# Attention heads: three value pairs in one burst, pair sums in the second head's burst, reciprocal in two halves

## The reference

```python
s = jnp.einsum('bqhd,bkhd->bhqk', q, k, preferred_element_type=jnp.float32) * (QK_DIM ** -0.5)
pr = jax.nn.softmax(s, axis=-1).astype(v.dtype)
return jnp.einsum('bhqk,bkhd->bqhd', pr, v)
```

## Time and profile before

| | |
|---|---|
| median of 3 runs | 1334.23 us (1332.66 to 1334.96) |
| profiled execution, its time | 1332.62 us |
| its span, first to last instruction | 1330.8 us |
| busy in the span | PE 1312.5 us, DVE 683.3, ACT 467.9, POOL 433.5 |
| chain that ended last | PE 94%, DVE 3%, DMA 1%, ACT 1% |
| mean granted TensorE clock | 0.993 of full |
| attention heads, first score tile to projection | 278.93 to 368.28 us |

### The profile page before, as it was taken

How to read it: one execution, slowest core, us unless ns; L and a number is a source line. 1 busy time by engine, 2 the same in 40 slices (tenths; PEclk the granted TensorE clock), 3 DMA queues, 4 the chain that set the end, 5 groups by cost and what they waited for, 6 DMA issues and landing times.

```text
span 1330.8 us, 15819 instructions
## 1 busy us (share of the span) xinstructions
PE 1312.5 (99%) x6356; PEld 966.1 (73%) x6356; DVE 683.3 (51%) x1253; ACT 467.9 (35%) x629; POOL 433.5 (33%) x136
## 2 busy tenths in 40 slices
PE   8999999999999999999999999999999999999998
PEld 5789888865578844444447788888888888888887
DVE  2465987767783633333347756712461451551553
ACT  4335222346631221112135671433242341431443
POOL 3143334247712000000015334444245345344340
PEclk9999999999999799999999999999999999999999
DMA  9521199301024799999993113222132222223201
GB/s 374 219 96 64 47 357 328 122 1 64 32 96 190 273 366 420 421 420 421 421 400 127 64 64 127 96 96 95 64 127 95 96 95 95 95 95 103 87 1 64
DMA packets 33924, 226.69 MB, mean 170 GB/s; under 512 B 4000, under 2 KB 4640, under 8 KB 7872
## 3 DMA queue, kind: packets, MB, share of 16 engines
q1 hardware_dynamic: 32416, 218.93, 42.9%
q0 software_dynamic: 1152, 4.19, 0.9%
q10 hardware_dynamic: 288, 2.62, 0.5%
HBM read 221.53 MB, written 4.19 MB: 170 GB/s over the span
## 4 chain that ended last, share of the span: by engine, by line
PE 94%; DVE 3%; DMA 1%; ACT 1%; issue 0%; POOL 0%; SPq 0%; DVEq 0%; ACTq 0%
PE psum L964 24%; PE psum L966 23%; PE psum L965 23%; PE psum L1468 13%; PE psum L1276 1%; PE psum L1242 1%; PE psum L1453 1%; PE psum L1456 1%; DMA raw<-in_stream 1%; PE psum L1540 1%; PE psum L1428 1%; PE psum L1011 1%; DVE rs L2447 1%; PE psum L1016 0%; DVE work L2578 0%
## 5 line engine op out<-in xcount | busy, mean ns | idle before, releaser
L898 POOL TENSOR_TENSOR w_lo<-raw,w_hi 128x2048 fp32r<-128x2048 f32 x79 | 365.2, 4624 | 589.6 <-ACT w_hi L1741 589.6
L964 PE MATMUL psum<-b_hi,w_hi 128*128 128x512 f32 x608 | 238.1, 392 | 0.1
L966 PE MATMUL psum<-b_hi,w_lo 128*128 128x512 f32 x608 | 236.7, 389 | 0.0
L965 PE MATMUL psum<-b_lo,w_hi 128*128 128x512 f32 x608 | 236.6, 389 | 0.0
L1741 ACT ACTIVATE w_hi<-raw 128x2048 fp32r<-128x2048 f32 x80 | 152.6, 1908 | 147.8 <-PE psum L966 101.8
L964 PEld LDWEIGHTS psum<-b_hi,w_hi 128*128 128x128 f32 x608 | 114.1, 188 | 30.7 <-issue 5.7
L966 PEld LDWEIGHTS psum<-b_hi,w_lo 128*128 128x128 f32 x608 | 114.1, 188 | 23.9
L965 PEld LDWEIGHTS psum<-b_lo,w_hi 128*128 128x128 f32 x608 | 114.1, 188 | 23.3
L1468 PE MATMUL psum<-ex_ring,xe 128*64 128x512 f32 x488 | 108.8, 595 | 0.9 <-ACT xe L1966 0.9
L2495 DVE TENSOR_TENSOR x<-psum,x 128x512 f32<-128x512 f32 x39 | 26.9, 692 | 127.9 <-PE psum L966 127.9
L964 PE MATMUL psum<-h_hi,w_hi 128*128 128x512 f32 (+1 forms) x208 | 84.4, 406 | 1.3 <-POOL w_lo L881 1.3
(11 more groups left out here) (432 smaller groups left out, 2294.3 us busy)
## 6 DMA issues: line engine op xcount, KB each, us to landing
raw<-in_stream SPq DMA_DIRECT2D x97, 1024.0 KB, 4.9
ex_ring<-in_stream SPq DMA_DIRECT2D x89, 1024.0 KB, 17.7
mod_in<-in_stream SPq DMA_DIRECT2D x8, 1024.0 KB, 20.7
ex_last<-in_stream SPq DMA_DIRECT2D x7, 1024.0 KB, 17.3
x<-in_x SPq DMA_DIRECT2D x4, 512.0 KB, 7.1
x<-in_x ACTq DMA_DIRECT2D x1, 2048.0 KB, 7.6
xt<-h2t SPq DMA_DIRECT2D x8, 256.0 KB, 10.5
out<-y_out SPq DMA_DIRECT2D x4, 512.0 KB, 3.0
```

The costliest lines, as they stand in the source:

```text
L898: nc.gpsimd.tensor_tensor(w_lo[:, slot, :], raw[:, raw_slot, :], w_hi[:, slot, :].bitcast(F32), ALU.subtract).then_inc(w_lo_done, 1)
L964: mm(o, w[0], x[0], start=start, stop=False)
L965: mm(o, w[0], x[1], start=False, stop=False)
L966: return mm(o, w[1], x[0], start=False, stop=stop)
```

## The change

On TensorE the last value pair of a head moves into the burst behind its own score tiles, which then has three pairs. The sums of a pair of heads follow that burst at the end of heads 1, 3, 5 and 7, in bank 1. On ACT the copy of the sums becomes two copies of 256 columns, behind the row of maxima of heads 1, 3 and 5, ahead of the next head's high parts; the copy of the values' result comes after the second exponential. On VectorE a pair's reciprocal and multiply are made in two halves of 256 tokens, the first at the end of heads 2, 4, 6, the second at the end of heads 3, 5, 7, and both for the last pair after head 7. GpSimd's code is unchanged.

```diff
@@ make_plan
             p.add("sT", h, k, by="act", bank=k % 3)
-            if k == 2 and h >= 2 and h % 2 == 0:
-                p.add("sums", h // 2 - 1, by="act", bank=5)
             if k >= 2 and h + 1 < H:
                 max_pair(h + 1, k - 2)
+        if h % 2 == 1:
+            p.add("sums", h // 2, by="act", bank=1)
         if h + 1 < H:
             p.add("mx_row", h + 1, by="act", bank=0)
@@ tensor
-                    if k == 2 and h >= 1:
-                        pv_pair(h - 1, KT - 2)
-                        if h % 2 == 0:
-                            prob_sums(h // 2 - 1)
                     if k >= 2 and h + 1 < H:
                         max_pair(h + 1, k - 2)
-                pv_pair(h, 0)
-                pv_pair(h, 2)
+                for k in range(0, KT, 2):
+                    pv_pair(h, k)
+                if h % 2 == 1:
+                    prob_sums(h // 2)
                 if h + 1 < H:
                     max_row(h + 1)
...
-            pv_pair(H - 1, KT - 2)
-            prob_sums(H // 2 - 1)
@@ scalar
                 if j >= 1:
-                    act.wait_ge(att_done, j)
-                A(rs[:], o, ACT.Copy).then_inc(freed_act, 1)
+                    act.wait_ge(att_half, j)
+                A(rs_first[:], o[:, 0:FH], ACT.Copy)
+                if j >= 2:
+                    act.wait_ge(att_done, j - 1)
+                A(rs_second[j % 2][:], o[:, FH:T], ACT.Copy).then_inc(freed_act, 1)
...
-                    if k == 2 and h >= 1:
+                    if k == 1 and h >= 1:
                         output(h - 1)
-                        if h % 2 == 0:
-                            output_sums(h // 2 - 1)
...
                 if h + 1 < H:
                     max_row(h + 1)
+                    if h % 2 == 1:
+                        output_sums(h // 2)
@@ vector
+            def pair_output(j, s):
+
+                if s == 0:
+                    dve.wait_ge(freed_act, PLAN.freed_count(TILE["sums", j]))
+                    dve.wait_ge(o_sum, 2 * j + 2)
+                r, tok = (rs_first, rs_second[j % 2])[s], slice(s * FH, s * FH + FH)
+                link(V.reciprocal(r[:], r[:]))
+                V.tensor_tensor(att[:, j, tok], att[:, j, tok], r[:], ALU.mult).then_inc((att_half, att_done)[s], 1)
...
-                if h >= 2 and h % 2 == 0:
-                    pair_output(h // 2 - 1)
+                if h >= 2:
+                    pair_output(h // 2 - 1, h % 2)
...
-            pair_output(H // 2 - 1)
+            for s in range(2):
+                pair_output(H // 2 - 1, s)
```

More of the change, by code:

```diff
@@ L375, in make_plan @@
             head_t(h + 2)
-    p.add("sums", H // 2 - 1, by="act", bank=5)
     p.phase(6)
@@ L591, in build @@
         att = at("att", R + 34, [P, 4, T])
-        rs = at("rs", R + 98, [P, T])
+        rs_first = at("rs_first", R + 98, [P, FH])
+        rs_second = [at("rs_second0", R + 99, [P, FH]), at("rs_second1", R + 31, [P, FH])]
         att_hi = at("att_hi", R + 80, [P, 4, T], F32R)
@@ L731, in build @@
         psum_done = sem("psum_done")
+        att_half = sem("att_half")
         att_done = sem("att_done")
```

## The result

The changed kernel takes 1336.48 us in the median of its 20 runs against 1332.1 us; the ratio is 1.0027 (95% interval 1.0019 to 1.0034), 3.6 us slower. One run took 4632.58 us for a reason that nothing here shows, and is not in the ratio. The profiled execution has a span of 1332.9 us against 1330.8. Spans of one kernel spread by some us. The two traces differ in the granted clock of the routing stage after attention (0.85 from 425 to 444 us in the trace of before, 1.00 in that of after over the same work), and what follows attention took 1.3 us less in that of after. It was 278.93 to 368.28 = 89.35 us and is 279.26 to 371.69 = 92.43 us: +3.08.

A forecast was written before the change was run, and what follows sets the result against it. The prediction took TensorE, busy for 99% of the span, as the bound. Its terms came to +1.14 us, plus 2.06 for held multiplies, so +3.2 on 1334.2 gave 1337.4 us, range 1333.5 to 1340.5.

The forecast's parts named there:

- The lone pair goes: Heads 1, 3, 5, before the burst: without the single value pair TensorE waits for VectorE's low parts; saves 4.76 us.
- Copies ahead of the high parts: Start of heads 2, 4, 6 on ACT: two half copies add 0.72 us; head still saves 1.27 each, 3.81 us.
- t0: Clock of a head: the start of its row of maxima on TensorE (L1255).
- B: Clock of a head: the start of its burst of value products on TensorE (L1276).
- K: End of VectorE's low parts of k in a head; forecast t0+3.90 in odd heads, t0+4.62 in even before meetings.
- Third pair: Bursts of heads 0 to 6: the third value pair adds 0.86 us each, 6.02 us.
- Sums at the end of heads 1, 3, 5: Behind these bursts: sums add 2.58 us, and waiting for GpSimd's fifth addition adds 0.37 three times, 1.11 us.
- rival A: Heads 3 and 5: second-half multiply gets ahead of GpSimd's weight chunk or isn't held; +1.1, 1335.4 us; chance 0.22.
- Where the second halves land: Multiplies of heads 3 and 5 held by GpSimd's weight chunk, delaying heads 4 and 6 by 1.03 us each, +2.06.
- rival B: Not slower: ACT copies and GpSimd's fifth addition hidden, no multiply held; -2.1, 1332.1 us; chance 0.10.
- Head 7, "nothing gained": Last head: the lone pair goes, but the sums wait for GpSimd's additions, so nothing is gained.
- Rival C: More meetings: head 7's half reciprocal and multiply, and later low parts of attention, delay sums; +4.6, 1338.8 us; chance 0.18.

The follow-up runs named there:

- burst_halves_wait: Changed kernel with sums and copies put back, GpSimd waiting for the second half's multiply before weight chunks after heads 3 and 5: 1330.46 us, ratio 0.9983.
- burst_only: Kernel before with only the value pairs' part, three pairs in one burst, sums and whole reciprocal as before: ratio 1.0002.
- after_dve_copies: Changed kernel with GpSimd waiting for the second half's multiply, and the first three pairs' sums copied by VectorE instead of ACT: ratio 1.0007.
- after_pe_fifth: Changed kernel with the fifth addition of heads 1, 3, 5 taken from GpSimd, TensorE adding that term in the sums: ratio 1.0015.
- after_bank5: Changed kernel with the last pair's sums in bank 5 instead of bank 1: ratio 1.0014.

## Why the prediction was right, and where it was not

The direction and size came out: +3.2 forecast, +3.08 in the stage, +3.6 by the ratio. Its terms did not all hold, and the total owes part of its closeness to luck.

- *The lone pair goes* (4.76 us saved in heads 1, 3, 5): 1.18+1.89+1.89 = 4.96. Right. `burst_halves_wait`, without the moved sums, gives the same 7.87, 7.88 and 7.85; `burst_only`, which keeps the whole reciprocal ahead of the low parts, gives it in head 1 alone (heads 3 and 5 at 8.91 and 8.90), as the reason given in brackets says.
- *Copies ahead of the high parts* (8.65 us in even heads): 8.48 and 8.45, each 0.2 less. VectorE's low parts of k in head 2 ended at 303.60+1.32 = 304.92, t0+4.50 instead of 4.62:

```profile
303.60 1.32 DVE L2421 SCALAR_TENSOR_TENSOR k_lo<-psum,cols,k_hi 96x512 fp32r<-96x512 f32 x2
```

  `after_dve_copies` shows the term itself, 0.59 us a head against 0.72. The wait of the first score tile was there (0.36 us instead of some 0.7), and B still follows K by 3.98, as in head 1 by 3.96, so it was free, as said.
- *Third pair* (0.86 seven times): 2.73-1.87. Right, with no gap in the burst.
- *Sums at the end of heads 1, 3, 5*: mis-sized. Behind the burst I had 0.37+0.86 each; heads 1, 3, 5 took 4.21, 4.62 and 4.26, so 1.48, 1.89 and 1.53: 4.90 us in all against 3.69. The waits from the end of the burst were 0.48, 0.88 and 0.52 instead of 0.37, and the sums themselves took 1.00 instead of 0.86 after a wait. In heads 1 and 5 the sums started at t0+11.06 and t0+11.11, near the forecast's 11.03; in head 3 at t0+11.48. For head 3 the step that failed is "against: the addition chain's step has been the same in every head", in rival A: head 3 has a pause of 0.49 to 0.50 us ahead of one of its additions in the trace of before, in that of after and in every run's but `after_pe_fifth`'s. After shows it above (320.28, released by its own previous addition). It stood on GpSimd's timeline of before, and I had read only head 1's:

```profile
319.28 1.28 POOL L921 TENSOR_TENSOR psum_odd<-psum_odd,probs 128x512 f32<-128x512 f32 x1 [0.49 <-POOL psum_odd L921]
```

- *Where the second halves land* (two meetings, 2.06): one meeting, 0.93. Multiply and chunk started at t0+11.23 and t0+11.29 in head 3, and at t0+11.22 and t0+10.92 in head 5. So the pause in head 3 let the multiply go ahead. For that head rival A was right, for head 5 the forecast. The price of a meeting, 1.03 forecast, is near; the forecast's own terms give K = t0+5.7, not 5.65, and so 1.1. The sign that went with it, a TensorE wait of near 2 us ahead of L1242 in heads 4 and 6 and up to 1 in head 2, came as 0.64 us in head 6 (352.42 above) and as no row in heads 2 and 4. Its absence was to speak for rival B, and as a sign it was badly chosen: the copies cost 0.59 us in heads 2 and 4 all the same (`after_dve_copies`), with a wait of 0.36 us ahead of the first score tile.
- *Head 7, "nothing gained"*: wrong by 0.6. I followed the last sums to GpSimd but not the bank: the projection opens banks 0 to 3, and the sums now lay in bank 1 until ACT had copied them. The plan of before had these sums in bank 5, and its trace has none of this wait; the plan's line in the diff gave the new bank. `after_bank5` measures it as 0.82.
- *Rival C*: the second half's multiply in head 7 did meet the additions (at 366.15, 1.53 us long), but the last sums start 8.07 us after the head's first tile against 8.36 before (366.42 less 358.06). It had no price.

So the forecast was 1.1 us too high for the meetings and 0.8 too high ahead of the bursts (0.2 in heads 1, 3 and 5, 0.6 in the even heads). It was 1.2 us too low at the three sums and 0.6 too low in head 7, where it had no wait at the projection. These errors cancel to 0.1 us. The mechanisms that it named were there, but that the total came so near is luck.

The forecast of the time itself, 1337.4 us, started from 1334.2 for the kernel before; in the comparison that kernel took 1332.1.

## What to carry to other kernels

Before moving work out of a gap, ask what it covers: the lone pair looked like a switch to be saved, and it was hiding some 0.3 us of the low parts of k in a head and, in head 7, over a microsecond of GpSimd's additions. When two operations on different engines can exclude each other, their order in time is part of the design: an explicit wait on the engine with slack took the ratio from 1.0015 to 0.9983. For a moved PSUM tile, check the next user of its new bank, and read the pace of a helper engine in every repetition, not in one.

## What the runs showed of the hardware

Waits of 2.17 and 2.14 us on TensorE went with 6.8 and 3.4 us at half clock in the two executions seen; the fall came 0.3 us before it started again in the first and 0.4 us after in the second. Waits of 1.50 us in the same place were not followed by a fall. A held multiply of 256 columns ended about 0.3 us after GpSimd's chunk in every case (346.52+4.53 = 351.05, chunk to 350.77), and VectorE's reciprocal, with one SBUF input, was never lengthened: 1.73 to 1.75 us for 256 columns with GpSimd busy or not. GpSimd pauses 0.5 us ahead of the fourth addition of head 3 in eleven of the twelve traces. In `after_pe_fifth`, where GpSimd makes one addition fewer in head 1, the fourth addition of head 3 is there and the pause is not, so that head's own work up to there doesn't bring it by itself. Why it comes stays open.
